# A two-layer transformer kernel in float32: 37 constant products on TensorE are left out

## What is computed

```
hx = modulate(rms_norm(x, norm_g[layer, 0]), sh1, sc1)
ox, oc = mixer(hx, hc, ...)                    # ends in a product with w_out
x = x + g1 * ox
hx = modulate(rms_norm(x, norm_g[layer, 1]), sh2, sc2)
pg = softmax(hx @ wg + bg); gi = argmax(pg)
le = (hx @ we + be) of group gi; tw, ti = top_k(softmax(le), 2)
y = sum of the 2 chosen experts:  (silu(gate) * up) @ w_down, weighted
x = x + g2 * y
```

## Time and profile before

| | |
|---|---|
| median of 3 runs | 2736.35 us |
| the profiled execution's own time | 2734.06 us |
| its span | 2732.3 us |
| mean granted TensorE clock | 0.986 |
| TensorE busy | 2631.3 us (96%) |
| VectorE busy | 1020.3 us (37%) |
| ScalarE, GpSimd busy | 545.4 us (20%), 229.7 us (8%) |
| DMA | 586.07 MB, mean 215 GB/s |

### The profile page before, as it was taken

One profiled execution on the slowest core, in us unless ns is written; L12 is line 12 of the kernel. 1 busy time (PEld: TensorE's weight loads), 2 busy tenths in 40 slices (PEclk: granted clock), 3 DMA queues, 4 the chain that ended last, 5 costly groups with the idle time before them and its releaser, 6 DMA issues.

```text
span 2732.3 us, 34317 instructions
## 1 busy us (share of the span) xinstructions
PE 2631.3 (96%) x13604; PEld 1330.3 (49%) x13604; DVE 1020.3 (37%) x2420; ACT 545.4 (20%) x1137; POOL 229.7 (8%) x339
## 2 busy tenths in 40 slices
PE   6999999999999999999999799899999899999996
PEld 3444456556755544433333354477755444444442
DVE  3222337107745642222222362387745611111114
ACT  3201111117821100000000130188831100000001
POOL 0011200003011110000000000000011110000000
PEclk9999999999999999999999999999999999999998
DMA  9641110206050289999998810200030599999996
GB/s 365 251 189 34 36 43 24 74 0 121 2 234 31 93 308 421 427 388 392 407 382 347 345 62 31 50 20 1 2 134 31 220 377 425 416 424 406 413 413 240
DMA packets 97194, 586.07 MB, mean 215 GB/s; under 512 B 20296, under 2 KB 23584, under 8 KB 72072
## 3 DMA queue, kind: packets, MB, share of 16 engines
q1 hardware_dynamic: 80616, 535.71, 50.1%
q0 software_dynamic: 13824, 38.68, 3.6%
q10 hardware_dynamic: 2592, 9.44, 0.9%
HBM read 553.93 MB, written 41.79 MB: 218 GB/s over the span
## 4 chain that ended last, share of the span: by engine, by line
PE 90%; DMA 5%; DVE 2%; issue 1%; SPq 1%; ACT 0%; POOL 0%; PEld 0%; PEldq 0%; DVEq 0%; POOLq 0%; ACTq 0%
PE PS L1819 35%; PE PS L940 24%; PE PS L1475 9%; PE PS L1290 4%; PE PS L1302 4%; PE PS L1313 4%; DMA ar<-in_expert_w_gu_dram 2%; PE PS L1824 2%; DMA ar<-in_ada_w_dram 1%; PE PS L584 1%; PE PS L1829 1%; PE PS L2228 1%; PE PS L1494 1%; DMA ar<-in_x_dram 1%; PE PS L912 1%
## 5 line engine op out<-in xcount | busy, mean ns | idle before, releaser
L1819 PE MATMUL PS<-ar 128*32 128x512 f32 (+2 forms) x4608 | 1011.8, 596 | 13.3 <-DMA ar<-in_expert_w_gu_dram 6.7
L940 PE MATMUL PS<-ar 128*128 128x512 f32 (+1 forms) x1600 | 674.3, 577 | 0.2 <-issue 0.2
L1819 PEld LDWEIGHTS PS<-ar 128*32 128x32 f32 (+2 forms) x4608 | 370.4, 137 | 617.6 <-issue 609.3
L940 PEld LDWEIGHTS PS<-ar 128*128 128x128 f32 x1600 | 298.9, 190 | 330.4 <-issue 325.5
L1475 PE MATMUL PS<-ar 128*128 128x512 f32 x576 | 254.3, 595 | 0.6 <-DVEq L421 0.6
L1943 ACT ACTIVATE ar<-PS 128x512 f32<-128x512 f32 x48 | 28.7, 598 | 1052.4 <-PE PS L1819 1052.4
L1344 DVE CUSTOM_DVE_ANT_0 ar<-PS,ar 128x640 f32<-128x640 f32 (+2 forms) x208 | 158.0, 797 | 203.6 <-POOL ar L1260 133.5
L1475 PEld LDWEIGHTS PS<-ar 128*128 128x128 f32 x576 | 106.9, 190 | 122.8 <-issue 122.0
L1399 ACT ACTIVATE ar<-ar 128x641 f32<-128x641 f32 (+4 forms) x208 | 160.0, 775 | 0.8 <-DVE ar L1344 0.8
L2036 DVE TENSOR_TENSOR ar<-PS,ar 128x1024 f32<-128x1024 f32 x48 | 58.8, 1225 | 245.1 <-PE PS L1819 140.0
L2013 DVE TENSOR_TENSOR ar<-PS,ar 128x512 f32<-128x512 f32 x48 | 33.2, 692 | 313.5 <-ACT ar L1943 313.5
(11 more groups left out here) (240 smaller groups left out, 1808.7 us busy)
## 6 DMA issues: line engine op xcount, KB each, us to landing
ar<-in_expert_w_gu_dram SPq DMA_DIRECT2D x128, 2048.0 KB, 15.0
ar<-in_expert_w_down_dram SPq DMA_DIRECT2D x64, 2048.0 KB, 15.8
ar<-in_ada_w_dram SPq DMA_DIRECT2D x24, 2048.0 KB, 13.1
ar<-yd SPq DMA_DIRECT2D x36, 512.0 KB, 7.1
ar<-in_ab_w_in_dram SPq DMA_DIRECT2D x7, 2048.0 KB, 8.6
h2d<-ar ACTq DMA_DIRECT2D x18, 512.0 KB, 2.6
ar<-in_swa_w_in_dram SPq DMA_DIRECT2D x3, 2048.0 KB, 10.7
ar<-mod SPq DMA_DIRECT2D x3, 1536.0 KB, 7.8
```

The source lines that it names most:

```text
L940: mm = nc.tensor.matmul(out_, lhs, rhs, start=(k == 0), stop=(k == KC - 1))
L1819: mm = nc.tensor.matmul(out[at:to], lhsT[:, at:to], w[:, k, cols], start=start, stop=stop)
```

## The change

All calls of running, and the function, are removed. Nothing else differs.

```diff
@@ n1_pe
                 tr.then_inc(S(f"n1_tr{l}"), 1)
-            if l == 1:
-                running(9)
             turn(0)
...
-        def running(n, bank=0):
-
-            for _ in range(n):
-                nc.tensor.matmul(PS[:, bank, :], ident, cst[:, 0:512], start=True, stop=True)
-
@@ out_pe
                 if 1 <= i <= len(ts):
                     turn2(i - 1)
-                if i >= len(ts):
-                    running(3)
                 if i >= 2:
                     ranks(i - 2)
                 if i < len(ts):
                     product(i, 1)
                 if 1 <= i <= len(ts):
                     router(i - 1)
-                if i == len(ts) + 1:
-                    running(1)
                 if i >= 2:
                     places(i - 2)
@@ moe_pe
-            running(6)
             turn(0)
-            running(1, bank=2)
             for b in range(nb):
                 gate(b)
```

## The result

The changed kernel takes 2751.58 us, the median of 5 runs (2749.07 to 2751.87 but for one run of 8000.39, which the ratio leaves out), against 2736.68 us for the kernel before. The ratio is 1.0046, with a 95% interval of 1.0034 to 1.0058: slower by some 12.6 us, between 9 and 16. The forecast was 2747.8, in a range of 2740 to 2753, with 0.87 on slower.

The account below looks back on a forecast made before the run. Bound by where TensorE's work (96% busy) stands on the chain and its clock. Tail, join and clock terms sum to 11.4 us on the profiled 2734.06, 2745.5; with 2.3 to the runs' median, 2747.8, range 2740 to 2753.

Parts of the forecast that it names:

- The clock falls without the fillers and stays down through both tails: Both routing tails: granted clock 0.50 from the last transposes to some 3 to 5 us behind the first expert product.
- Logits +1.7 and +1.8: Last tile's logits in the tails: later by 1.7 us (layer 0) and 1.8 us (layer 1), rank products and router slower.
- the second case: Both tails: router keeps its pace, logits only some 0.3 us late; +8.5 us in all, 2744.9; chance 0.20.
- Gate(0) +1.85 and +3.4: First expert product starts later behind the choice: 1.85 us in layer 0, 3.4 us in layer 1.
- The 1.28 us that turn(0) of layer 0 could have won: Tail of layer 0: without running(6), turn(0) could start 1.28 us sooner, but the later gather eats it.
- The join +0.7: Between the layers: turn(1) at half clock, first projection product starts 0.7 us later; turn(0) starting sooner gains 0.
- The clock's return: First expert product of each layer and first projection product: each begins at half clock and loses 1.8 us.
- The sign named: In the new profile, the clock comes back some 3 to 5 us behind the first expert product, in both layers.
- The bounds of 1.76 and 2.3: Limits in us for a dense product's loss at half clock, from a layer 1 expert group and the fillers at 956.21.
- The sum: Whole kernel: 1.85 + 1.8 + 3.4 + 1.8 + 0.7 + 1.8 = 11.4 us slower.
- The third rival: Clock returns later, 2.3 instead of 1.8 us at three places, plus one more fall, 1.76: +14.6, 2751; chance 0.08.
- The not-slower rival: TensorE stays at 2.4 GHz through the tails, clock 1.0 when gate(0) starts; -1.3 us, 2735.0; chance 0.07.

Follow-up runs that it names:

- thin_short: The kernel before with its fillers at all their places, each product of 512 columns replaced by two of 32 columns; 1.0046, 12.6 us slower.

## Why the prediction was right, point by point

- **The clock falls without the fillers and stays down through both tails.** Right: 0.50 from the router to behind the first expert product in both layers. thin_short shows that the full queue is not what counts, and the records show what the clock costs: sixteen router records 3.61 us instead of 1.95, eight transposes 1.98 instead of 1.17.
- **Logits +1.7 and +1.8.** Measured 4.64 instead of 2.75 and 2.64: +1.9 and +2.0. The load rows of half clock gave the router's price; sixteen records at 0.214 are the 3.43 on the chain, for 3.5 forecast. The rest is the rank products ahead of it: 1.07 us (0.64 and 0.43 on the chain) for the 0.85 taken. With that the second case (the router keeps its pace) falls: at half clock the loads last 333 ns instead of 190. By the Trainium skill's rule (TensorE: Matmul & The Clock Gate, LDWEIGHTS), that a load takes its columns over 1.2 GHz, the sixteen would have kept their pace; the trace does not agree, they took 3.61 us instead of 1.95.
- **Gate(0) +1.85 and +3.4.** Measured +2.1 and +3.65. Of the parts, the places of layer 1 took 1.13 instead of 0.67, and turn(0) 1.99 and 1.98 at half clock where 1.86 was taken. The 1.28 us that turn(0) of layer 0 could have won were indeed eaten by the later gather: it waited for it (967.12). But that these 1.28 us were there to be eaten was a matter of the one profile that was read: where running(6) runs at full clock (35.5 and 35.7 us to gate(0) in the experiments, against 39.3 in the changed kernel), the same change costs 3.6 to 3.8 us in layer 0 and not 2.1. Which of the two the median of the kernel before contains more of is not shown.
- **The join +0.7, no gain from the freer turn(0).** Measured +0.65 from turn(1) on.
- **The clock's return, 1.8 at each of three places.** This is the term that was mis-sized: 3.0, 1.4 and 1.1 in the first profile, 5.5 together where 5.4 was forecast, so the errors cancelled, and that is luck. The sign named, the clock back some 3 to 5 us behind the start of the product, was met at none of the three: 6.1, 2.9 and 2.5 us. The bounds of 1.76 and 2.3 were too narrow: 1.1 to 3.0 was seen for the same instructions, and 10.16 and 8.66 us for the same product in two executions.
- **The sum.** 11.4 us against 12.6 and 14.0 by the two paired measurements, inside both intervals. The absolute forecast of 2747.8 is 3.8 below the median, 2.8 without the run of 8000.39. By the first profile 3.6 us lie in stretches that the change does not touch; whether the medians' rest lies there too is not shown. The steady groups of the expert stage kept their 20.95.
- **The third rival** (2.3 us at each of the three places and one more fall, +14.6, 2751) is not told apart by the time: 14.6 lies inside both intervals too, and 2751 is nearer to the median. The places speak for neither figure: 3.0 is above 2.3, 1.4 and 1.1 are below 1.8. The one more fall was there (8.40 instead of 6.95), but the kernel before had one of its own that this profile lacks (22.71 against 21.02).
- **The not-slower rival** (the clock doesn't need them) had 0.07 and is refuted at the number it named: the clock at gate(0) was 0.50.

## What to carry to other kernels

A product that computes nothing can be worth its time when TensorE's next real work stands on the chain, and what it is worth can be read before it is tried: find rows of the same instructions at both clocks, and add up the ones on the chain. It must be wide (512 columns here; 32 did nothing), and must end before what it waits beside: at half clock a record of it takes up to 1201 ns instead of 592, and then it stands in the way itself (running(6) with 8.2 us instead of 5.4; sixteen products at the end with 16.8). Count a filler by the shortest gap at the slow clock, not by the mean gap at the fast one.

## What the runs showed of the hardware

- Narrow work back to back does not bring the clock back: 5.00 of 5 us busy with products of 32 columns at 0.50, and sixteen router records of 36 columns ran through at 0.50. Products of 512 columns brought it back, and so did transposes of 128 columns (0.79, then 1.00). The Trainium skill (TensorE: Matmul & The Clock Gate, Part 4) says of transposes that the full clock does not engage for them; in this float32 form the granted clock did reach 1.00. Whether its records, which show as MATMUL, use the mode that the page means, no run here shows.
- The first dense product lost 1.1 to 3.0 us, with the clock back 2.5 to 6.1 us behind its start, for like instructions. Behind a wait of 2.6 us the clock fell in one profile and behind one of 2.5 us at the same place it did not in another (22.71 and 21.02 us for the same group); behind 3.0 us it held in one and behind 3.1 us at the same place it fell in the other (6.95 and 8.40). A forecast of one such place can be off by more than 1 us (1.8 was taken, 3.0 came).
- The time of a 128-column float32 weight load follows the granted clock: 186 to 192 ns at 1.00, 333 at 0.50.
